# One tile fewer in the index part of a sparse attention mixer: index key and weights share a tile, and ropes, key copy and top-k rounds are reordered

## The chip, the cores and the metric

The kernel runs on one core of a Trainium2 chip. The metric is the device time of one execution in microseconds, as the median of several executions. The profile shows one execution, instruction by instruction, on TensorE (PE), VectorE (DVE), ScalarE (ACT), GpSimd (POOL) and SyncE (SP), which only issues DMAs here.

## The reference

Two transformer blocks are applied to 512 tokens of width 1024. The first has a windowed attention, a convolution and a cross attention between two feed-forward parts. The second has two layers; the first of them is the mixer that matters here:

```python
def _dsa_mixer(h, positions, w_in, q_norm_g, k_norm_g, idx_k_ln_g, idx_k_ln_b, w_out):
    proj = h @ w_in          # q 1024, k 256, v 256, qi 512, ki 64, wi 8 columns
...
    q = _rope(_rmsnorm(q, q_norm_g), positions)
    k = _rope(_rmsnorm(k, k_norm_g), positions)
    qi = _rope(qi, positions)
    ki = _rope(_layernorm(ki, idx_k_ln_g, idx_k_ln_b)[:, :, None, :], positions)[:, :, 0, :]
    wi = wi * (IDX_HEADS ** -0.5 * IDX_DIM ** -0.5)
...
        s = jnp.einsum('bqhd,bsd->bqhs', qib, ki)
        score = jnp.einsum('bqhs,bqh->bqs', jax.nn.relu(s), wib).astype(jnp.float32)
...
        _, sel = lax.top_k(score, topk)      # topk = 128
```

An index of 8 heads (queries `qi`, one shared key `ki`, weights `wi` per head) scores every earlier token for each query; the 128 best are kept, and the 16 query heads attend to these alone. `h` is a normed and modulated `x` with a shift added: `h = rmsnorm(x) * (1 + sc) + sh`.

## The kernel before

**Layout.** Activations stand feature by token: a tile is 128 features by 512 tokens. A float32 product is made of three passes, high times high, low times high and high times low, over 8 chunks of 128 rows, so a tile's job is 24 matmuls with 512 moving columns. Weights come by SP in a ring of four slots (`w_raw`); ScalarE makes the high part (`w_hi`, line 1223), and VectorE (line 1587) or, in the mixers, GpSimd (line 619, two halves) the low part. SP loads the tile j only after the split of the tile j-4.

**The mixer's tiles.** `TILES_B` lists 18 tiles of the stage `mixB`: `ki` (the 64 key columns twice, for both halves of the partitions), `wi` (8 columns), `qi0` to `qi3`, `vB0`, `vB1`, `kB0`, `kB1` and `qB0` to `qB7`. A job m computes tile m into bank m mod 4; `freed` makes it wait until the tile four before has left the bank. Between the chunks, behind chunks 2 and 5 (parts 0 and 1), `betweenB(m, part)` puts small matmuls on TensorE.

**The first two tiles.** `first_two` computes `ki` and `wi` from raw `x` before the norm is known, interleaved chunk by chunk. Their results are then scaled by the norm on VectorE (lines 2056 and 2057), and a bias, the shift times the weights, is added on ScalarE. That bias starts as eight operations per tile on VectorE, `shift_through` (lines 1627 and 1630), whose width is that of the tile, 128 and 8, in the last steps of the stage before; TensorE sums it over the partitions (line 752) ahead of the first product. Tile 2 and those after it use the normed `h`, chunk by chunk as it is made.

**The key's chain.** `ki` is centred (a total by matmul, line 1151), squared, summed (`head_sum`), its root taken on ScalarE (`head_std`), inverted on VectorE (`head_rstd`, line 1836), spread over partitions by 16 matmuls (`head_spread`, line 943, bank 5), multiplied in (`head_norm`) and roped. All spreads use bank 5, so the spread of one key waits until the norm of the key before is done (`h_normed`).

**Ropes.** `head_rope` is three VectorE operations: tile times cosine (line 1855), the tile with its halves swapped times sine (line 1857), and their sum (line 1859). The swapped tile comes by four DMAs on SP (`swap_halves`), issued in `mixer` in a fixed order between the weight loads: `qi` and `qB` seven loads behind their own, the keys nine, `ki` ten. `step_of_rope` says in which step m VectorE does it: two behind the tile for queries, four for keys, step 6 for `ki`. Staging for queries is a ring of two, so ScalarE's scaling of a query waits for the sine product of the query two before.

**Index and top-k.** `index_slot(m, part)` gives the two (block, head) pairs that TensorE scores in a part (line 1140); ScalarE applies the relu, VectorE weighs and sums it (lines 2067 and 2070). The pairs begin in job 6, part 1, and end in job 12, part 0. `take_top` is one of 16 rounds of each of three blocks of queries (256, 384 and 512 columns): the 8 largest (line 2082) and their replacement (line 2084). `TOPS_AT` says how many rounds stand ahead of the index sums of each part of a step: `{8: (0, 1), 9: (4, 1), 10: (5, 2), 11: (4, 1), 12: (0, 2), 13: (3, 0), ...}`, 33 in all; the other 15 come one per step in the attention from its step 7 on. In step m, VectorE inverts the key tile m-2 first (`head_rstd`) and norms it last (`head_norm`).

**The waits of GpSimd.** Its splits of `mixB` wait for chosen VectorE results (`qi3` roped, index sums, each `qB` roped).

## Time and profile before

| what | us |
|---|---|
| median of 3 runs | 2119.54 |
| the three runs | 2114.94, 2119.54, 2120.14 |
| profiled execution | 2114.27 |
| its span, first to last instruction | 2112.1 |
| TensorE busy in the span | 2093.0 |
| VectorE busy | 1242.8 |
| ScalarE busy | 783.1 |
| GpSimd busy | 298.9 |
| mean granted TensorE clock | 0.999 |

The span is what the trace covers; the execution's own time is 2.2 us longer. Matmul durations in the trace overlap, because each next one starts while the last one drains, so the pitch of starts tells what a matmul costs. A bracket at the end of a row is idle time of the engine ahead of it and what ended it. The stage `mixB` with its first two tiles covers about 931 to 1061 us, the attention behind it 1061 to 1169.

### The profile page before, as it was taken

The page shows a single profiled execution, that of the slowest core. Times are in us where ns is not written, and L with a number is a line of the kernel's source. Part 1 is how long each engine was busy: PE and PEld are TensorE (multiplying, and loading weights), DVE is VectorE, ACT ScalarE, POOL GpSimd, SP SyncE. Part 2 cuts the span into 40 slices and gives each one's busy share as a digit, 9 for nine tenths or more (in the row PEclk, how much of TensorE's full clock was granted, in tenths as well). Part 3 has the DMA queues.
Part 4 walks back from the last instruction along what each step waited for, and adds up shares of the span by engine and source line. Part 5 has one row for each costly group of instructions (what it writes and reads, how often), then busy time and mean ns, then how long its engine had stood idle before and what let it go on. Part 6 is the DMA issues. An engine that isn't in the chain of part 4 may idle for free.

```text
span 2112.1 us, 28230 instructions
## 1 busy us (share of the span) xinstructions
PE 2093.0 (99%) x9964; PEld 1718.3 (81%) x9968; DVE 1242.8 (59%) x1839; ACT 783.1 (37%) x1087; POOL 298.9 (14%) x357
## 2 busy tenths in 40 slices
PE   9999999999999999999999999999999999999999
PEld 7888888887888888877777888888888878888887
DVE  7666544786676654466995676654466456333332
ACT  6222333557442223334365442223343234222222
POOL 0122400650212230024300212210000000000000
PEclk9999999999999999999999999999999999999999
DMA  5556233320345542323300346542333222222232
GB/s 192 181 194 197 91 110 110 118 94 2 110 163 188 197 136 82 97 94 115 109 22 1 105 155 199 186 145 81 97 100 110 97 82 100 99 90 99 76 96 87
DMA packets 79572, 243.33 MB, mean 115 GB/s; under 512 B 12784, under 2 KB 13424, under 8 KB 79376
## 3 DMA queue, kind: packets, MB, share of 16 engines
q1 hardware_dynamic: 61376, 189.61, 27.5%
q0 software_dynamic: 18128, 52.84, 8.0%
q8 instruction: 40, 0.66, 0.1%
q14 instruction: 28, 0.23, 0.0%
HBM read 235.84 MB, written 2.29 MB: 113 GB/s over the span
## 4 chain that ended last, share of the span: by engine, by line
PE 92%; DVE 5%; ACT 1%; issue 1%; POOL 1%; DMA 0%; SPq 0%; ACTq 0%; DVEq 0%; POOLq 0%
PE ps L710 28%; PE ps L712 28%; PE ps L711 28%; PE ps L1014 2%; PE ps L972 1%; PE ps L993 1%; DVE ps L1980 1%; DVE tmp L1630 1%; DVE small L1876 1%; PE ps L975 0%; PE ps L1140 0%; POOL w_lo L619 0%; PE ps L917 0%; DVE qA L1859 0%; DVE ropA L1857 0%
## 5 line engine op out<-in xcount | busy, mean ns | idle before, releaser
L710 PE MATMUL ps<-h_hi,w_hi 128*128 128x512 f32 x1888 | 740.5, 392 | 2.8 <-issue 1.5
L712 PE MATMUL ps<-h_hi,w_lo 128*128 128x512 f32 x1888 | 735.4, 390 | 0.0
L711 PE MATMUL ps<-h_lo,w_hi 128*128 128x512 f32 x1888 | 735.2, 389 | 0.0
L1587 DVE TENSOR_TENSOR w_lo<-w_raw,w_hi 128x1024 fp32r<-128x1024 f32 x336 | 411.4, 1226 | 382.5 <-ACT w_hi L1223 368.0
L1223 ACT ACTIVATE w_hi<-w_raw 128x1024 fp32r<-128x1024 f32 x383 | 402.2, 1052 | 242.5 <-PE ps L712 240.7
L710 PEld LDWEIGHTS ps<-h_hi,w_hi 128*128 128x128 f32 x1888 | 353.8, 187 | 83.5 <-issue 8.8
L712 PEld LDWEIGHTS ps<-h_hi,w_lo 128*128 128x128 f32 x1888 | 353.7, 187 | 74.7
L711 PEld LDWEIGHTS ps<-h_lo,w_hi 128*128 128x128 f32 x1888 | 353.9, 187 | 73.1 <-issue 0.2
L710 PE MATMUL ps<-hid_hi,w_hi 128*128 128x512 f32 x704 | 274.1, 389 | 0.0
L711 PE MATMUL ps<-hid_lo,w_hi 128*128 128x512 f32 x704 | 274.0, 389 | 0.0
L712 PE MATMUL ps<-hid_hi,w_lo 128*128 128x512 f32 x704 | 274.0, 389 | 0.0
L619 POOL TENSOR_TENSOR w_lo<-w_raw,w_hi 128x512 fp32r<-128x512 f32 x100 | 132.7, 1347 | 531.4 <-ACT w_hi L1223 482.9
L1300 ACT ACTIVATE hid_hi<-tmp 128x512 f32 (+1 forms) x88 | 55.6, 632 | 393.6 <-DVE tmp L1763 384.8
L710 PEld LDWEIGHTS ps<-hid_hi,w_hi 128*128 128x128 f32 x704 | 132.2, 188 | 27.6
L711 PEld LDWEIGHTS ps<-hid_lo,w_hi 128*128 128x128 f32 x704 | 132.2, 188 | 27.3
L712 PEld LDWEIGHTS ps<-hid_hi,w_lo 128*128 128x128 f32 x704 | 132.2, 188 | 27.3
L1763 DVE TENSOR_TENSOR tmp<-tmp,ps 128x512 f32<-128x512 f32 x83 | 57.0, 687 | 132.3 <-PE ps L712 132.3
L1297 ACT ACTIVATE tmp<-ps 128x512 f32<-128x512 f32 x83 | 49.6, 598 | 223.4 <-PE ps L712 223.4
L1698 DVE SCALAR_TENSOR_TENSOR ada_sum<-ada_raw,c_act,ada_sum 128x512 f32<-128x512 f32 x168 | 125.9, 749 | 6.0 <-DMA ada_raw<-in_ada_w 1.8
L588 POOL DMA_DIRECT2D ada_raw<-in_ada_w x96 | 52.7, 549 | 393.5 <-DVE ada_sum L1698 372.8
L1704 DVE TENSOR_TENSOR hid_lo<-tmp,hid_hi 128x512 f32 (+1 forms) x88 | 61.4, 698 | 77.0 <-ACT hid_hi L1300 77.0
L1233 ACT ACTIVATE tmp<-x 128x512 f32 (+1 forms) x56 | 35.3, 631 | 158.1 <-DVE x L1609 157.7
(308 smaller groups left out, 1757.2 us busy)
## 6 DMA issues: line engine op xcount, KB each, us to landing
ada_raw<-in_ada_w POOLq DMA_DIRECT2D x96, 512.0 KB, 4.9
w_raw<-in_gate SPq DMA_DIRECT2D x88, 512.0 KB, 4.0
w_raw<-in_up SPq DMA_DIRECT2D x88, 512.0 KB, 3.5
w_raw<-in_down SPq DMA_DIRECT2D x64, 384.0 KB, 3.1
w_raw<-in_down SPq DMA_DIRECT2D x64, 320.0 KB, 2.8
w_raw<-in_w_mix_c SPq DMA_DIRECT2D x24, 512.0 KB, 3.4
w_raw<-in_w_mix_b SPq DMA_DIRECT2D x17, 512.0 KB, 3.5
w_raw<-in_w_mix SPq DMA_DIRECT2D x16, 512.0 KB, 3.5
```

The source lines that it names most:

```text
L588: pool.dma_start(ada_raw[:, (piece % 2) * 2 * ADA:(piece % 2 + 1) * 2 * ADA], src.rearrange("a p n -> (a p) n")).then_inc(ada_in[piece % 2 ...
L619: low = pool.tensor_tensor(w_lo[:, at:at + WT // 2], w_raw[:, at:at + WT // 2], f32(w_hi[:, at:at + WT // 2]), ALU.subtract)
L710: pe.matmul(dest, s_hi, m_hi, start=first and n == 0, stop=False)
L711: pe.matmul(dest, s_hi, m_lo, start=False, stop=False)
L712: mm = pe.matmul(dest, s_lo, m_hi, start=False, stop=last and n == len(pairs) - 1)
L1223: act.activation(chunk(w_hi, slot, WT), chunk(w_raw, slot, WT), ACT.Copy).then_inc(w_hi_done, 1)
L1297: act.activation(chunk(tmp, u), bank(s), ACT.Silu).then_inc(silu_done, 1)
L1300: act.activation(hid_hi[:, bass.ds(i * (2 * T) + u * T, T)], chunk(tmp, 2 + u), ACT.Copy)\
L1587: dve.tensor_tensor(chunk(w_lo, slot, WT), chunk(w_raw, slot, WT), f32(chunk(w_hi, slot, WT)), ALU.subtract).then_inc(w_lo_done, 1)
L1698: dve.scalar_tensor_tensor(ada_sum[:, :], w, c_act[:, k:k + 1], ada_sum[:, :], ALU.mult, ALU.add).then_inc(ada_sum_done, 1)
L1704: dve.tensor_tensor(hid_lo[:, at], chunk(tmp, 2 + u), f32(hid_hi[:, at]), ALU.subtract)\
L1763: dve.tensor_tensor(chunk(tmp, 2 + u), chunk(tmp, u), bank(s), ALU.mult)\
```

## The change

`ki` and `wi` share one tile: 64 key columns, 8 weight columns and 56 of zeros. The `wi` tile goes, so there are 17 jobs, and `qi0` becomes the second tile of `first_two`, computed from raw `x`, scaled by VectorE and given its bias by ScalarE. The key is handled on 64 partitions, and once normed is copied to the other 64 by a fifth DMA, for which its rope waits. The DMAs of `qi` are issued six loads behind their own instead of seven, the key's nine instead of ten; the key is roped in step 5, behind `qi2`, and its spread (8 matmuls) moves to part 1 of job 4. Index pairs begin in job 6, part 0. `kB0` and `kB1` are inverted one step earlier, behind the sums of part 0, and the table of rounds is new, with 32 rounds instead of 33 ahead of the attention. `shift_through` for the second tile is 128 wide.

```diff
-        TILES_B = ["ki", "wi", "qi0", "qi1", "qi2", "qi3", "vB0", "vB1", "kB0", "kB1"] + [f"qB{t}" for t in range(8)]
+        TILES_B = ["ki", "qi0", "qi1", "qi2", "qi3", "vB0", "vB1", "kB0", "kB1"] + [f"qB{t}" for t in range(8)]
...
         def shift_sum(n, s):
-            return tmp[:, 3 * T + s * P:3 * T + s * P + (8 if n == 3 and s == 1 else P)]
+            return tmp[:, 3 * T + s * P:3 * T + (s + 1) * P]
...
             if t == "ki":
-                return 6
+                return 5
...
-            return rot_key[t], 64
+            return rot_key[t], 80 if t == "ki" else 64
...
         def turn_bank(t):
+            if t == "wi":
+                return bank(7)[:, HD:HD + TT * 8]
...
-        TOPS_AT = {8: (0, 1), 9: (4, 1), 10: (5, 2), 11: (4, 1), 12: (0, 2), 13: (3, 0), 14: (3, 0), 15: (3, 0), 16: (3, 0),
-                   17: (1, 0)}
+        TOPS_AT = {8: (1, 4), 9: (1, 5), 10: (2, 4), 11: (1, 0), 12: (2, 0), 13: (3, 0), 14: (3, 0), 15: (3, 0), 16: (3, 0)}
...
-            at = 4 * (m - 6) + 2 * part - 2
-            return IDX[max(at, 0):at + 2] if 0 <= at < len(IDX) else []
+            at = 4 * (m - 6) + 2 * part
+            return IDX[at:at + 2] if 0 <= at < len(IDX) else []
...
+                if t == "ki":
+                    sp.dma_start(kraw[HD:P, :], kraw[0:HD, :]).then_inc(rot_sem(t)[0], 16)
...
-                    due = [t for t in tiles if has_rope(t) and j == tiles.index(t) + {"q": 7, "k": 10 if t == "ki" else 9}[t[0]]]
+                    due = [t for t in tiles if has_rope(t) and j == tiles.index(t) + {"qi": 6, "qA": 7, "qB": 7}.get(t[:2], 9)]
...
             for j in range(LEAD, len(TILES_B) + KC):
+                if j == 8:
+                    after(pool, h_roped, "qi3")
                 if j == 9:
-                    after(pool, h_roped, "qi3")
+                    after(pool, i_sum, (1, 5))
                 if j == 10:
-                    after(pool, i_sum, (1, 5))
-                if j == 11:
                     after(pool, i_sum, (2, 1))
-                if 15 <= j <= 20:
-                    after(pool, h_roped, f"qB{j - 15}")
+                if 14 <= j <= 19:
+                    after(pool, h_roped, f"qB{j - 14}")
...
-                if part == 0 and m == 5:
+                if part == 1 and m == 4:
                     head_spread("ki")
-                if part == 0 and TILES_B[m - 2] in h_normed.value and m > 4:
+                if part == 0 and TILES_B[m - 2] in h_normed.value and m > 2:
                     head_spread(TILES_B[m - 2])
...
+            after(act, d_misc, "qi_scaled")
+            act.activation(straight("qi0"), straight("qi0"), ACT.Identity, bias=shift_out(3, 1)).then_inc(h_scaled.at("qi0"), 1)
             lead(J + 1)
...
+                if t == "ki":
+                    dve.wait_ge(*rot_sem(t))
                 dve.tensor_tensor(chunk(rop, 0), straight(t), tab_cos, ALU.mult)
...
-            dve.tensor_tensor(kraw[:, :], bank(0), ssum[:, :], ALU.mult).then_inc(d_misc.at("ki_scaled"), 1)
-            dve.tensor_tensor(relu[0:8, 0:T], bank(1)[0:8, :], ssum[0:8, :], ALU.mult).then_inc(d_misc.at("wi_scaled"), 1)
+            dve.tensor_tensor(kraw[0:HD, :], bank(0)[0:HD, :], ssum[0:HD, :], ALU.mult).then_inc(d_misc.at("ki_scaled"), 1)
+            dve.tensor_tensor(features_of("wi"), bank(0)[HD:HD + 8, :], ssum[HD:HD + 8, :], ALU.mult)\
+                .then_inc(d_misc.at("wi_scaled"), 1)
+            dve.tensor_tensor(straight("qi0"), bank(1), ssum[:, :], ALU.mult).then_inc(d_misc.at("qi_scaled"), 1)
...
                 n = "ki" if m == 4 else TILES_B[m - 2]
-                if n in h_rstd.value and m > 4:
-                    head_rstd(n)
-                if m == 4:
+                if m == 3:
                     after(dve, a_misc, ("tabB", "cos"))
...
                     for b, h in index_slot(m, part):
                         index_sum(b, h)
+                    if part == 0 and TILES_B[m - 1] in ("kB0", "kB1"):
+                        head_rstd(TILES_B[m - 1])
                 if n in h_normed.value and m > 3:
                     head_norm(n, straight(n))
...
-    main = tiles(np.concatenate([ki, ki, qi, vv, k, q], axis=1))
-    wt = np.zeros((1, P, WT), np.float32)
-    wt[:, :, :KC * 8] = tiles(wi, 8)
-    a["w_mix_b"] = np.concatenate([main[0:1], wt, main[1:]], axis=0)
+    room = np.zeros((D, P - HD - 8), np.float32)
+    a["w_mix_b"] = tiles(np.concatenate([ki, wi, room, qi, vv, k, q], axis=1))
```

## Rows read from the trace of the kernel before

**Rows 1.** Page, part 1: busy time, share of the span and instructions.

```profile
PE 2093.0 (99%) x9964; PEld 1718.3 (81%) x9968; DVE 1242.8 (59%) x1839; ACT 783.1 (37%) x1087; POOL 298.9 (14%) x357
```

**Rows 2.** Windows: length, busy time per engine, granted clock, DMA share, GB/s.

```profile
977.60:1061.20 83.60, 82.91 (x426) 63.10 (x426) 74.53 (x163) 34.01 (x59) 31.59 (x24) 1.00 0.33 102
```

**Rows 3.** Timeline around the shift sums: start us, duration, engine, line, operation, idle before.

```profile
927.51 3.70 DVE L1630 SCALAR_TENSOR_TENSOR tmp<-w_raw,modc,tmp 128x8 f32<-128x8 f32 x7
...
928.09 2.57 POOL L619 TENSOR_TENSOR w_lo<-w_raw,w_hi 128x512 fp32r<-128x512 f32 x2 [0.65 <-ACT w_hi L1223]
...
931.26 0.51 PE L752 MATMUL ps<-ones,tmp 128*128 128x1 f32 x4 [0.95 <-DVE tmp L1630]
...
1561.70 2.67 DVE L1630 SCALAR_TENSOR_TENSOR tmp<-w_raw,modc,tmp 128x128 f32<-128x128 f32 x7
```

**Rows 4.** Timeline of TensorE: the first two tiles, and first products of jobs.

```profile
944.22 0.40 PE L711 MATMUL ps<-h_lo,w_hi 128*8 128x512 f32 x1
...
945.36 0.39 PE L710 MATMUL ps<-h_hi,w_hi 128*128 128x512 f32 x1
...
950.80 0.39 PE L710 MATMUL ps<-h_hi,w_hi 128*128 128x512 f32 x1
...
991.80 0.39 PE L710 MATMUL ps<-h_hi,w_hi 128*128 128x512 f32 x1
```

**Rows 5.** Timeline of TensorE: work put between the products of the jobs.

```profile
965.51 1.09 PE L943 MATMUL ps<-identity,hrB 128*64 128x128 f32 x16
...
974.24 0.70 PE L1140 MATMUL ps<-ki,qi 64*128 64x256 f32 x4
...
1002.32 1.09 PE L943 MATMUL ps<-identity,hrB 128*64 128x128 f32 x16
...
1004.33 0.92 PE L1140 MATMUL ps<-ki,qi 64*128 64x384 f32 x4
...
1012.14 1.09 PE L943 MATMUL ps<-identity,hrB 128*64 128x128 f32 x16
...
1060.09 1.05 PE L917 MATMUL ps<-matsB,hsB 128*128 128x2 f32 x8 [0.69 <-ACT hsB L1343]
```

**Rows 6.** Timeline of VectorE in the tiles of the mixer.

```profile
962.47 1.24 DVE L1857 TENSOR_TENSOR ropB<-pTB,ada_raw 128x512 f32<-128x512 f32 x1 [7.05 <-DMA pTB<-qnB]
...
996.19 2.30 DVE L2070 SCALAR_TENSOR_TENSOR score<-relu,wi,score 128x384 f32<-128x384 f32 x2 [0.30 <-ACT relu L1551]
...
1001.61 0.43 DVE L2082 MAX8 top<-score 128x8 f32<-128x256 f32 x1
...
1002.60 0.43 DVE L2082 MAX8 top<-score 128x8 f32<-128x256 f32 x1
...
1005.80 1.34 DVE L2070 SCALAR_TENSOR_TENSOR score<-relu,wi,score 128x384 f32<-128x384 f32 x2 [0.29 <-ACT relu L1551]
...
1010.50 0.68 DVE L1849 TENSOR_TENSOR pB<-pB,ps 128x512 f32<-128x512 f32 x1
...
1021.40 0.68 DVE L1855 TENSOR_TENSOR ropB<-pB,ada_raw 128x512 f32<-128x512 f32 x1
...
1023.51 0.69 DVE L1855 TENSOR_TENSOR ropB<-qnB,ada_raw 128x512 f32<-128x512 f32 x1
...
1060.74 0.69 DVE L1859 TENSOR_TENSOR qB<-ropB 128x512 f32<-128x512 f32 x1
...
1061.53 0.55 DVE L1863 RECIPROCAL qinv<-qstd 128x64 f32<-128x64 f32 x1
```

**Rows 7.** Timeline of the DMA queue and of GpSimd.

```profile
958.21 2.46 SPq L552 DMA_DIRECT2D pTB<-qnB  x4
...
992.16 5.19 POOL L619 TENSOR_TENSOR w_lo<-w_raw,w_hi 128x512 fp32r<-128x512 f32 x4 [4.31 <-DVE score L2070]
```

**Rows 8.** Timeline of VectorE in the attention: the max of a round.

```profile
1073.36 0.69 DVE L2082 MAX8 top<-score 128x8 f32<-128x512 f32 x1
```

**Rows 9.** Windows, columns as in rows 2: the stretch at low clock.

```profile
1063.00:1064.00 1.00, 1.00 (x7) 1.00 (x7) 0.97 (x4) 0.91 (x4) 0.00 (x0) 0.50 0.54 129
```

More of the change, by code:

```diff
@@ L760, in first_two @@
                         for s in range(2 * pair, 2 * pair + 2):
-                            width = 8 if n == 3 and s == 1 else P
-                            mm = product(None, bank(s)[0:width, :], [(weights(js + s, k, width),
-                                                                       (chunk(hi, k), chunk(lo, k)))], k == 0, k == KC - 1)
+                            mm = product(None, bank(s), [(weights(js + s, k), (chunk(hi, k), chunk(lo, k)))],
+                                         k == 0, k == KC - 1)
                             if k == KC - 1:
@@ L856, in freed @@
                     after(pe, v_done if tiles is TILES_B else evac, t)
-                elif t == "ki" or t[0] == "g":
+                elif t == "ki":
+                    after(pe, d_misc, "wi_scaled")
+                elif t[0] == "g":
                     after(pe, evac, t)
@@ L888, in tile_job, with turn_tile @@
                         between(m, 1)
-            def turn_tile(tiles, m):
-                t = tiles[m]
+            def turn_tile(t):
                 after(pe, evac, t)
-                if tiles is TILES_A and t != "vA":
+                if t in TILES_A and t != "vA":
                     after(pe, v_done, "vA" if t == "mv0" else "mv0")
@@ L925, in head_sum @@
                 for b in range(MT if t[:2] == "mk" else TT):
-                    mm = pe.matmul(bank(4)[:, at + 2 * b:at + 2 * b + 2],
-                                   hs[:, (n % 2) * T + b * P:(n % 2) * T + (b + 1) * P], mats[:, P:2 * P:HD],
-                                   start=True, stop=True)
+                    if t == "ki":
+                        squares, heads = hs[0:HD, (n % 2) * T + b * P:(n % 2) * T + (b + 1) * P], mats[0:HD, P:P + 2]
+                    else:
+                        squares, heads = hs[:, (n % 2) * T + b * P:(n % 2) * T + (b + 1) * P], mats[:, P:2 * P:HD]
+                    mm = pe.matmul(bank(4)[:, at + 2 * b:at + 2 * b + 2], squares, heads, start=True, stop=True)
                 mm.then_inc(sq_read.at(t), 1)
@@ L941, in head_spread @@
                 for b in range(MT if t[:2] == "mk" else TT):
-                    for half in range(2):
+                    for half in range(1 if t == "ki" else 2):
                         mm = pe.matmul(bank(5)[half * HD:(half + 1) * HD, b * P:(b + 1) * P],
@@ L1133, in index_pair @@
                     after(pe, h_roped, "ki")
+                    after(pe, v_done, "wi")
                 if pair[0][0] == 1:
@@ L1150, in betweenB @@
                     after(pe, evac, "ki")
-                    pe.matmul(bank(6), matsB[:, P:2 * P], kraw[:, :], start=True, stop=True)\
+                    pe.matmul(bank(6)[0:HD, :], matsB[0:HD, P:P + HD], kraw[0:HD, :], start=True, stop=True)\
                         .then_inc(p_misc.at("ki_total"), 1)
                 if part == 1 and m == 3:
-                    turn_tile(TILES_B, 1)
-                if part == 0 and is_token_major(TILES_B[m - 1]) and m > 2:
-                    turn_tile(TILES_B, m - 1)
+                    turn_tile("wi")
+                if part == 0 and is_token_major(TILES_B[m - 1]):
+                    turn_tile(TILES_B[m - 1])
                 if part == 0 and has_norm(TILES_B[m - 1]):
@@ L1515, in _ @@
             after(act, d_misc, "ki_scaled")
-            act.activation(kraw[:, :], kraw[:, :], ACT.Identity, bias=shift_out(3, 0)).then_inc(evac.at("ki"), 1)
+            act.activation(kraw[0:HD, :], kraw[0:HD, :], ACT.Identity, bias=shift_out(3, 0)[0:HD, :])\
+                .then_inc(evac.at("ki"), 1)
+            after(act, d_misc, "wi_scaled")
+            act.activation(features_of("wi"), features_of("wi"), ACT.Identity, bias=shift_out(3, 0)[HD:HD + 8, :])\
+                .then_inc(evac.at("wi"), 1)
+            after(act, d_misc, "qi_scaled")
+            act.activation(straight("qi0"), straight("qi0"), ACT.Identity, bias=shift_out(3, 1)).then_inc(h_scaled.at("qi0"), 1)
             lead(J + 1)
@@ L1522, in _ @@
                     head_square(t, hsB)
-                if t[:2] in ("qB", "qi"):
+                if t == "qi0":
+                    pass
+                elif t[:2] in ("qB", "qi"):
                     head_scale(t, col("g_q2") if t[:2] == "qB" else 1.0, straight(t))
@@ L1526, in _ @@
                     head_gain(t, col("g_k2"), straight(t))
-                elif t == "wi":
-                    after(act, d_misc, "wi_scaled")
-                    act.activation(features_of(t), features_of(t), ACT.Identity, bias=shift_out(3, 1)[0:8, :])\
-                        .then_inc(evac.at(t), 1)
                 else:
```

36 lines of the change are left out of this document (20 added, 16 removed).

## The prediction

> **What bounds the kernel now.** I read the page first: TensorE is busy 99% of the span [rows 1]. So whatever takes matmuls off TensorE can be worth its full time, as long as TensorE does not wait instead. Then I read the stretch from 977.6 to 1061.2 us, where most of the mixer with the index runs: TensorE is busy for 82.9 of 83.6 us and VectorE for 74.5 [rows 2]. Both numbers matter. TensorE sets the pace, but VectorE, which has the top-k rounds, is close behind. Last I read the timelines of VectorE, TensorE, GpSimd and the DMA queue around the tiles that the change touches. The reader is to see there how far behind TensorE the vector work runs, since the change takes time from TensorE and nearly none from VectorE.
>
> **The tile that goes.** The weights tile (8 columns) has 24 matmuls. With a stationary operand of 128x8 one takes 0.39 us by its row, as one of 128x128 does [rows 4]: the 512 moving columns set the time. A job of 24 takes 950.80 - 945.36 = 5.44 us [rows 4]. One job of 18 goes: -5.44 us of TensorE. The spread of the index key goes from 16 matmuls to 8; 16 take 1.09 us [rows 5], so -0.5. The matmul of the key's total keeps its 512 columns: 0. Weight bytes hardly move (a 32 KB tile goes, 17 of 512 KB stay), and one split on ScalarE and on GpSimd goes; neither engine is the bound. If nothing waited, the sum would be -5.9 us.
>
> **The shift sum.** VectorE multiplies the shift into the weights of the stage's first two tiles before TensorE may start. For the second tile this was 8 operations on 128x8 and becomes 8 on 128x128. TensorE waits on exactly this: it was idle 0.95 us until the last one had ended, at 931.26 [rows 3]. Undisturbed, seven on 128x128 take 2.67 us, 0.38 each [rows 3]. Of the seven on 128x8, two were held by GpSimd's splits at 928.09; the trace's 3.70 us are 5 of 0.24 and two of 1.2 [rows 3]. Wider operations lengthen the free five by 0.12 each: +0.6 us; if all eight lengthen by 0.14, +1.1. I take 0.6, because held ones end when GpSimd ends. Everything behind is later by it.
>
> Here a rule weighs in: the Trainium skill, GPSIMD Engine Reference, Specifications, says that GpSimd shares SBUF interfaces with VectorE and contends with instructions that have two SBUF inputs. The trace agrees: two sums on 384 columns took 2.30 us beside a GpSimd split and 1.34 without [rows 6, 7], and a sine product 1.24 us [rows 6].
>
> **Key by DMA, raw index query.** In the raw pair, VectorE and ScalarE each get one more 128x512 operation (about 0.6 us each by the rows of such operations [rows 6]); ScalarE's next split of weights is 1.3 us later (this one and the weights' bias now lie ahead of it). GpSimd's half is then ready some 0.8 us before TensorE takes that tile: hidden, and 0.5 us on the path if GpSimd is held. The rotation of a query is four DMAs that take the queue 2.46 us, and its sine product starts 962.47 - 958.21 = 4.3 us after the first issue [rows 6, 7]. qi0 is now issued at about 952.6 (behind its ScalarE operation), so rotated at 957; qi1 behind the next load at 957, rotated at 961.3 and roped at 962.6. VectorE's reciprocal for the key stands behind that rope, and TensorE now asks for it in chunk 5 of job 4, at 962.0. So TensorE waits 0.7 to 1.1 us (0.9), a wait that the trace does not have. The key is normed at 965.2; five DMAs (one more, and behind it in the queue stand qi3 and two loads) take 3.1 us, and the rope starts about 5 us behind, at 970.3, and ends at 972.4. TensorE comes to the first index pair at about 973 (before: 974.24 [rows 5]): 0, with half a microsecond to spare. The value tiles' turns and pairs only change places.
>
> **The rounds, which is where the gain goes.** Count now to the next place at which TensorE asks for a result of VectorE: the spread of kB1, job 10 part 0, which needs kB0 normed, since both use bank 5. In the kernel before (job 11 there), TensorE goes from the end of the index pair at 1004.33 + 0.92 = 1005.25 to the spread at 1012.14: 6.9 us [rows 5]. VectorE starts the sums at 1005.80 and norms kB0 from 1010.50, ending 1011.18, 1.0 ahead [rows 5, 6]. Between them stand two rounds. A round on 256 columns is 1002.60 - 1001.61 = 0.99 us [rows 6]. The new table has five rounds between them: 0.55 (pair to sum) + 1.3 (two sums) + 5 x 0.99 + 1.3 + 0.68 (norm) = 8.8 us, against 6.9 - 0.2 (a narrower pair) = 6.7 on TensorE. TensorE waits 2.1 us, and about 3 if a GpSimd split holds the second pair of sums, as it does by the order of ScalarE's splits. The reciprocals ahead of the rounds do not help, because the norm is behind the rounds.
>
> Where does this leave VectorE? The job with that pair is job 9 now. It starts at 991.8 [rows 4] + 0.6 (shift) + 0.9 (key wait) + 1.2 (net of turns, pairs, spreads and a sum that come earlier) = 994.5, so the pair ends at 999.6, and kB0 is normed at N = 1008.4 to 1009.4. Then TensorE does spread, sum and pair, 3.1 us [rows 5], VectorE adds 0.55 + 1.3, and its two rounds lie in that wait. At N + 5 = 1013.4 to 1014.4 it has done what it had done at 1011.2 before: 2.2 to 3.2 us later, not 5 earlier. It had waited for pairs in jobs 8 and 9, because few rounds now stand ahead of the sums. From there to the attention VectorE is without a gap: two ropes per kB tile and one per query at 2.1 us each (1021.40 to 1023.51) [rows 6]. It saves one round on 512 columns, moved into the attention: a max of 0.69 us [rows 8], its replace as long, and the mask's addition, 1.7 in all. Some 0.5 of order comes back. Last rope before: ends 1061.43, and the reciprocal of the queries starts at 1061.53 [rows 6]; now about 1061.5 to 1062.5.
>
> TensorE meets VectorE once more: at job 12 it needs the squares of qB2, which ScalarE makes behind relus that wait for VectorE's sums, which now stand behind two ropes (4.2 us). By the same steps VectorE has these at N + 19.7, ScalarE's square ends at N + 20.7, TensorE comes at N + 18.9: 1.8 us of waiting. The sum for TensorE up to the first scores: -5.9 + 0.6 + 0.9 + 2.6 + 1.8 = 0.0; for VectorE 0 to +1. The later of the two counts, as the first scores are 1061.15 on TensorE and the reciprocal at 1061.53: +0.5.
>
> **The moved round.** In the attention a round lies in every step from 7 on; step 22 gets one more, 1.4 us. TensorE's chunk there is bound by its own matmuls, with VectorE idle behind it: 0, and 0.7 if the mask is late for the first score on all keys.
>
> **Sum.** The profiled execution took 2114.27 us (span 2112.1, 2.2 around it): 2114.27 + 0.5 = 2114.8. The kernel's runs lie on two levels, 2114.3 and 2114.9, and 2119.5 and 2120.1, so its median of 2119.54 is 5.3 above the profiled one. With +0.5 on each level a new median is near 2115 or near 2120; I put down 2118.0, between them. A change of under 0.3% (6.4 us) can't be told from none in this kernel.
>
> **The rivals.** *A: TensorE is never kept waiting.* VectorE was busy only 89% of rows 2, had idled for 7 us ahead of 962.47, and its work starts earlier. If the waits at jobs 10 and 12 and the key's fell away, the change would be -5.9 + 0.6 = -5.3: 2109.0 profiled. Against it stands the count of five rounds. Chance 0.22. *B: slower, by the clock.* TensorE's granted clock was 0.50 in 1063 to 1064 (1.2 of 2.4 GHz) [rows 9]. Ahead of it TensorE had stood still for 0.69 us and then done only small matmuls, on 2 and 128 columns [rows 5]. The waits of 2 to 3 us at job 10 are followed by just such ones. A half-speed stretch like that one, some 3.5 us, would lose 1.7 us of products; one at job 10 and one at job 12, 3.4: 2118.2 profiled. [...] The Trainium skill, TensorE: Matmul & The Clock Gate, on oscillation, says that idle gaps between bursts bring the slow clock back; by that rule B would hold. Against it: most of each stretch is dense products. Chance 0.12. *C: the key arrives late.* If DMAs of the key land 2 us later, the first pair waits 1.5 us and all index sums with it: 2116.3. Chance 0.08. That the tile stays is excluded by the diff.
>
> **How the numbers follow.** The likeliest has 0.58; its own range is -1 to +2 us (2113 to 2116.5 profiled, 2113 to 2122 with both levels). Range: A at the lower level and B at the upper give 2109 to 2123.5; I cut 1 in 10 on each side: 2110.5 to 2122.5. Faster by over 0.3% needs A, or a median at the lower level against one at the upper: 0.20. Slower by as much needs B with more than the two stretches, or the levels the other way: 0.08. Within: 0.72.
>
> **What would show it.** Right: 17 jobs; the wide shift sums and the first product about 0.6 later; a wait of TensorE at the spread of kB1 put down to VectorE's norm of some 2 to 3 us, one at a query sum of job 12 put down to ScalarE, one below a microsecond at the key's spread; first scores near 1061 to 1062. Wrong: if TensorE has no such wait and the first scores are near 1056, it is A; if the granted clock falls within the tiles, B. My weakest step is N, for it rests on the order of short VectorE operations; a rope or a round more or less there moves the result by 1 to 2 us.

## The result, and the profile after

The changed kernel takes 2122.13 us (median of 11 runs, 2118.76 to 2128.22), beside 2115.13 us for the kernel before in the same comparison (11 runs). The ratio is 1.0033, interval 1.0024 to 1.0042: slower by 0.33%, some 7 us, where I had forecast +0.5 and no change that can be told. In a later session it gave 2124.80 (5 runs) beside 2114.55, 1.0056 (1.0042 to 1.0069). The profiled execution took 2124.55 us, its span 2122.8. Two runs of the experiments below are far longer than all others (3910.16 us, the kernel before; 5910.35 us, the key's spread later) and are left out there.

The page's chain of work that ended last, its shares by engine, says where to look: VectorE has 8% of the chain, where it had 5% before.

```profile
PE 89%; DVE 8%; issue 1%; ACT 1%; DMA 0%; SPq 0%; POOL 0%; ACTq 0%; DVEq 0%
```

TensorE still is the bound, but it now stands in the chain behind VectorE more often. The timeline of the changed kernel shows each place (start, duration, engine, line, operation, idle time before it and what ended that). First the start of the mixer, as [rows 3, 5]:

```profile
926.77 4.49 DVE L1642 SCALAR_TENSOR_TENSOR tmp<-w_raw,modc,tmp 128x128 f32<-128x128 f32 x7
...
931.31 0.61 PE L755 MATMUL ps<-ones,tmp 128*128 128x1 f32 x4 [1.79 <-DVE tmp L1642]
...
957.61 1.67 DVE L1874 TENSOR_TENSOR qi<-ropB 128x512 f32<-128x512 f32 x1
959.38 1.58 DVE L1870 TENSOR_TENSOR ropB<-qnB,ada_raw 128x512 f32<-128x512 f32 x1
961.76 0.90 DVE L1872 TENSOR_TENSOR ropB<-pTB,ada_raw 128x512 f32<-128x512 f32 x1 [0.81 <-DMA pTB<-qnB]
962.70 1.64 DVE L1874 TENSOR_TENSOR qi<-ropB 128x512 f32<-128x512 f32 x1
...
964.50 1.09 PE L949 MATMUL ps<-identity,hrB 128*64 128x128 f32 x8 [1.66 <-DVE hrB L1848]
...
975.02 0.70 PE L1147 MATMUL ps<-ki,qi 64*128 64x256 f32 x4
```

The wide shift sums cost TensorE 1.79 us of idle time, where [rows 3] have 0.95. The key's spread is 8 matmuls, as it should be, but TensorE waits 1.66 us for the key's reciprocal. Above it stands why: three operations of the ropes ahead of that reciprocal took about 1.6 us each, beside GpSimd's splits (953.9 to 966.7), where the same ones take 0.69 undisturbed [rows 6]. Of these it is the last that the reciprocal waits for: between the first two and it VectorE was idle for 0.81 us, until the turned tile had landed by DMA. At 1.64 and 0.90 us instead of 0.69 each, the last two operations bring 1.2 us. The first index pair comes at 975.02, 0.8 us behind the 974.24 of before [rows 5] and 2 us behind my 973, and did not wait for the key.

Then the place where five rounds stand ahead of the norm of kB0, and what follows:

```profile
1001.66 1.34 DVE L2087 SCALAR_TENSOR_TENSOR score<-relu,wi,score 128x384 f32<-128x384 f32 x2 [1.58 <-ACT relu L1563]
...
1007.77 2.14 DVE L2087 SCALAR_TENSOR_TENSOR score<-relu,wi,score 128x384 f32<-128x384 f32 x2
1009.84 0.68 DVE L1862 TENSOR_TENSOR pB<-pB,ps 128x512 f32<-128x512 f32 x1
...
1010.66 1.09 PE L949 MATMUL ps<-identity,hrB 128*64 128x128 f32 x16 [2.81 <-DVE pB L1862]
...
1012.67 1.83 PE L1147 MATMUL ps<-ki,qi 64*128 64x512 f32 x4
...
1015.15 0.49 DVE L2084 TENSOR_SCALAR score<-relu,wi 128x512 f32<-128x512 f32 x1 [2.80 <-ACT relu L1563]
...
1028.32 4.28 DVE L2087 SCALAR_TENSOR_TENSOR score<-relu,wi,score 128x512 f32<-128x512 f32 x4
...
1032.12 1.05 PE L921 MATMUL ps<-matsB,hsB 128*128 128x2 f32 x8 [0.95 <-ACT hsB L1351]
...
1065.35 0.49 PE L978 MATMUL ps<-kB,qB 64*128 64x128 f32 x4
```

TensorE waits 2.81 us for the norm at the spread of kB1 (no wait in [rows 5]). VectorE, which made it wait, then waits 2.80 us itself for the next pair (1015.15), and TensorE again 0.95 us for ScalarE's squares at job 12. The pair behind the first wait took 1.83 us; undisturbed it is 1.13. Why, the windows say (length; busy time of PE, PEld, DVE, ACT and POOL; granted clock, DMA share, GB/s):

```profile
1010.00:1012.00 2.00, 1.34 (x19) 1.20 (x19) 1.90 (x7) 0.00 (x0) 1.05 (x1) 1.00 0.27 64
1012.00:1014.00 2.00, 2.00 (x11) 0.95 (x10) 0.36 (x1) 0.00 (x0) 0.00 (x0) 0.74 0.43 100
1014.00:1016.00 2.00, 2.00 (x6) 1.28 (x5) 0.74 (x2) 1.08 (x2) 0.00 (x0) 0.50 0.75 260
1016.00:1018.00 2.00, 2.00 (x9) 1.30 (x9) 1.90 (x7) 0.00 (x0) 0.00 (x0) 0.91 0.01 2
...
1034.00:1036.00 2.00, 2.00 (x6) 1.52 (x6) 1.86 (x4) 0.00 (x0) 0.00 (x0) 0.50 0.47 110
...
1158.00:1160.00 2.00, 0.83 (x7) 0.69 (x7) 0.94 (x3) 1.02 (x1) 0.00 (x0) 0.93 0.00 0
1160.00:1162.00 2.00, 2.00 (x12) 2.00 (x10) 0.77 (x1) 0.00 (x0) 0.00 (x0) 0.50 0.03 8
...
1166.00:1168.00 2.00, 2.00 (x12) 2.00 (x11) 0.00 (x0) 0.00 (x0) 0.00 (x0) 0.50 0.00 0
1168.00:1170.00 2.00, 2.00 (x7) 1.61 (x7) 0.94 (x3) 0.00 (x0) 0.00 (x0) 0.51 0.00 0
...
1714.00:1716.00 2.00, 2.00 (x6) 1.61 (x5) 0.00 (x0) 0.00 (x0) 0.00 (x0) 0.50 0.76 258
```

The third number from the end is TensorE's granted clock: 0.50 (1.2 of 2.4 GHz) behind the waits at 1010.66 and 1032.12, and again at 1158 to 1170 and 1712 to 1716. A window of 2 us at 0.50 loses 1 us of TensorE's work. Summed so over all windows, the four stretches lose 1.7, 1.7, 5.1 and 1.7 us, 10.2 together; 10.28 is what the profiled execution is longer than that of before. (A fifth, at the attention's start, is in both, 1.7 us each.) The last two lie behind waits that the change did not touch. Before had the same 1.17 us wait at the attention's end, and kept the clock (its timeline and its windows):

```profile
1155.19 1.09 PE L993 MATMUL ps<-matsB,pB 128*128 128x128 f32 x8 [1.17 <-ACT pTB L1397]
```

```profile
1158.00:1160.00 2.00, 2.00 (x20) 2.00 (x19) 0.00 (x0) 0.38 (x1) 0.00 (x0) 1.00 0.00 0
```

So in these two executions the waits and the saved tile nearly cancel, and the loss is clock: the first scores come at 1065.35, 4.3 us behind the 1061.08 of before, and 3.4 of that is the clock behind the waits at 1010.66 and 1032.12. One execution each is thin evidence, and the experiments had to tell whether the order of the rounds does it.

### The profile page after: what moved, and what is told of

Its sections match the earlier page's. It is cut to its first block, busy times and chain, and to the rows that moved or that the text cites. A ratio compares the mean times of both kernels' runs of the same rounds, so it can differ in the third digit from the quotient of the medians.

```text
span 2122.8 us, 28129 instructions
## 1 busy us (share of the span) xinstructions
PE 2098.9 (99%) x9932; PEld 1724.1 (81%) x9936; DVE 1246.7 (59%) x1840; ACT 782.6 (37%) x1086; POOL 298.8 (14%) x355
## 4 chain that ended last, share of the span: by engine, by line
PE 89%; DVE 8%; issue 1%; ACT 1%; DMA 0%; SPq 0%; POOL 0%; ACTq 0%; DVEq 0%
PE ps L713 28%; PE ps L715 27%; PE ps L714 27%; PE ps L1020 2%; DVE ps L1995 1%; PE ps L978 1%; PE ps L999 1%; DVE tmp L1642 1%; PE ps L981 1%; DVE small L1891 1%; DVE score L2101 0%; DVE top L2099 0%; DVE ropA L1872 0%; PE ps L1147 0%; DVE qA L1874 0%
```

## The experiments

Each was timed beside the kernel before (2114.85, 2114.55 and 2114.55 us in the three sessions). This table has for each the median, the mean, and the mean granted clock over its runs. From the clock follows an estimate of what it cost: (1 - clock) x 2118 us. It is a rough one. The clock of a run is recorded to 0.001, which is 2.1 us of it; and over the 196 runs, each kernel and session against its own mean, the time rises by only 0.8 us for each us of the estimate. So the last two columns tell where several us are, and not one.

| kernel | runs | median | mean | mean clock | lost by clock (estimate) | rest |
|---|---|---|---|---|---|---|
| before, the three sessions of the experiments | 76 | 2114.56 | 2115.1 | 0.9985 | 3.2 | 2111.8 |
| changed, both comparisons | 16 | 2124.34 | 2123.6 | 0.9952 | 10.2 | 2113.4 |
| changed, rounds early | 12 | 2116.26 | 2117.2 | 0.9966 | 7.2 | 2110.0 |
| before, norm late | 10 | 2120.02 | 2120.1 | 0.9977 | 4.9 | 2115.2 |
| fill of 18 and 7 | 10 | 2120.41 | 2121.9 | 0.9973 | 5.7 | 2116.2 |
| fill of 11 and 3 | 6 | 2122.08 | 2121.5 | 0.9970 | 6.4 | 2115.1 |
| fill in the attention | 12 | 2118.84 | 2119.5 | 0.9969 | 6.5 | 2113.0 |
| key's spread later | 5 | 2120.20 | 2121.1 | 0.9962 | 8.0 | 2113.0 |
| shift matmuls later | 5 | 2122.33 | 2122.3 | 0.9954 | 9.7 | 2112.6 |
| all four | 11 | 2110.43 | 2111.8 | 0.9985 | 3.3 | 2108.5 |
| all four, old table | 11 | 2116.99 | 2117.4 | 0.9969 | 6.5 | 2110.8 |
| all four, sums behind ropes | 11 | 2111.89 | 2112.2 | 0.9984 | 3.5 | 2108.7 |
| all four, with fill | 11 | 2109.69 | 2111.0 | 0.9984 | 3.5 | 2107.6 |

My theory going in: the order of the rounds makes TensorE wait, and the half clock behind the waits is part of their price. Rivals: VectorE's total work is the bound wherever its rounds lie; or the loss belongs to the attention's end.

**Rounds early.** The table alone:

```
-TOPS_AT = {8: (1, 4), 9: (1, 5), 10: (2, 4), 11: (1, 0), ...
+TOPS_AT = {8: (3, 3), 9: (2, 2), 10: (4, 3), 11: (1, 0), ...
```

> The changed kernel with another table of top-k rounds alone: 10 rounds ahead of the key's norm as before 11, but two between the last pair's sums and the norm of kB0, where the changed kernel has five; the others lie in VectorE's idle time ahead of the pairs. Theory (the order of the rounds makes TensorE's waits of 2.81 us at the spread of kB1 and about 1 us at job 12, and the half clock behind each, about 1.7 us, is their consequence): the wait at the spread falls below 0.5 us, the granted clock stays 1.00 in the tiles, first attention scores near 1060.5 instead of 1065.35, time 4 to 5 us below the changed kernel. Rival 1 (VectorE's whole work up to the attention is the bound, wherever the rounds lie): the wait only moves to a later job, first scores near 1064 to 1065, time unchanged. Rival 2 (the loss lies in the attention's end, where the clock was 0.50 for 10 us): the waits go, but the median stays within 2 us of the changed kernel.

Measured: 2116.26 us, 1.0008 (0.9995 to 1.0020) of before, so 5.9 and 8.5 us below the changed kernel's two medians, more than I expected. Two rounds now stand between the pair's sums and the norm, and the spread of kB1 follows the norm without a wait:

```profile
1006.64 1.34 DVE L2087 SCALAR_TENSOR_TENSOR score<-relu,wi,score 128x384 f32<-128x384 f32 x2 [0.61 <-ACT relu L1563]
...
1011.06 0.68 DVE L1862 TENSOR_TENSOR pB<-pB,ps 128x512 f32<-128x512 f32 x1
...
1012.76 1.09 PE L949 MATMUL ps<-identity,hrB 128*64 128x128 f32 x16
...
1032.54 1.05 PE L921 MATMUL ps<-matsB,hsB 128*128 128x2 f32 x8 [0.87 <-ACT hsB L1351]
```

VectorE's own wait for the next pair fell from 2.80 to 1.02 us. By the time, both rivals fall for this part: the work on VectorE is the same, and the attention's end was not touched. The first scores alone don't decide it. They were at 1064.19, where rival 1 had put them, not at 1060.5: in this execution the clock was at 0.50 behind the shift wait (2.11 us) and the key's (1.66 us), 5.1 us in all, and the wait at job 12 was still there, 0.87. At the attention's start the clock lost 6.8 us more, and with 2122.77 us the profiled run is the second longest of its twelve. The other waits seemed worth mending too.

**The same lateness put into the kernel before.**

```
-... 10: (5, 2), 11: (4, 1), ...
+... 10: (2, 5), 11: (4, 1), ...
```

> The kernel before with one entry of the table changed: of the seven rounds of its step 10, two ahead of the first pair's sums and five behind them, so that five stand between the sums and the norm of kB0, as in the changed kernel. Theory: TensorE waits 2 to 3 us at the spread of kB1 (no wait in the kernel before), the granted clock falls to 0.50 for 2 to 4 us behind it, worth 1 to 1.7 us; VectorE is idle 2 to 3 us ahead of that; time 3 to 5 us above the kernel before. Rival (such a wait is made good later, because VectorE and not TensorE sets the attention's start): 0 to 1 us. Rival (a wait costs only itself, the clock stays): 2 to 3 us.

Measured: 2120.02 us, 1.0022 (1.0013 to 1.0031), 5.2 above before, a little more than I expected, and all ten runs between 2118.86 and 2122.16. The timeline of the two engines and the windows:

```profile
1004.65 1.34 DVE L2070 SCALAR_TENSOR_TENSOR score<-relu,wi,score 128x384 f32<-128x384 f32 x2 [3.24 <-ACT relu L1551]
...
1012.99 0.68 DVE L1849 TENSOR_TENSOR pB<-pB,ps 128x512 f32<-128x512 f32 x1
...
1013.83 1.98 PE L943 MATMUL ps<-identity,hrB 128*64 128x128 f32 x16 [2.77 <-DVE hrB L1836]
```

```profile
1014.00:1016.00 2.00, 2.00 (x18) 1.67 (x18) 1.86 (x7) 0.00 (x0) 0.19 (x1) 0.50 0.28 66
...
1022.00:1024.00 2.00, 2.00 (x7) 1.16 (x7) 0.97 (x3) 0.00 (x0) 0.00 (x0) 0.50 0.03 8
```

VectorE stands idle for 3.24 us where it had rounds to do, TensorE then waits 2.77 us for it, and the clock is at 0.50 for 10 us behind that, 5.1 us lost. The profiled run is the longest of the ten (2122.16), though, and the others lost less: by the mean clock over the ten, 4.9 us against 3.2 of before, so 1.7 more, about one short stretch. The other 3.4 us of the difference of the means are the wait and what follows from it. This is the cleanest reading of the study: moving three rounds behind a pair of sums, no work added, costs about 5 us, where the wait itself is under 3. The rival "VectorE makes it good later" falls. "A wait costs only itself", 2 to 3 us, is not quite excluded by the interval (2.7 to 6.6 us), but the clock speaks against it.

**Filling the waits with matmuls of no use.** First 18 and 7, then 11 and 3:

```
+if part == 0 and m == 10:
+    after(pe, i_relu, (2, 7))
+    idle(18, 7)          # then 11
+if part == 0 and m == 12:
+    after(pe, h_normed, "kB1")
+    idle(7, 5)           # then 3
```

> The changed kernel with matmuls of no use on TensorE ahead of the two waits: 18 on 128 columns ahead of the spread of kB1 and 7 ahead of the query sum of job 12, each about 0.12 us at full clock, so 2.2 and 0.9 us inside waits of 2.81 and 0.95 to 1.4. Theory (the half clock behind the waits is due to TensorE's standing still): granted clock 1.00 through both places, the index pair behind the spread takes half of its 1.83 us, first scores 2 to 3.4 us earlier than 1065.35, time 2 to 3.4 us below the changed kernel. Rival (the clock falls from the mix of small matmuls there, or it falls for reasons outside of the kernel): clock 0.50 there all the same, time within 1 us of the changed kernel.

> As the kernel with 18 and 7 matmuls of no use ahead of the waits at the spread of kB1 and at job 12, but with 11 and 3: the profile of that kernel shows 36 passes in 4.18 us, so one takes 0.23 us, twice the price that I had put down, and its fill was 1.3 us longer than the wait. 11 and 3 take 2.5 and 0.7 us, inside the waits of 2.81 and 0.95. Theory (in the changed kernel the clock falls behind these waits and costs 1.7 us at each): no 0.50 there, mean granted clock over the runs as high as in the longer fill (0.9973, against 0.9955 of the changed kernel), median 1.5 to 3.5 us below the changed kernel's 2122.1, so 2118.6 to 2120.6. Rival: the median stays at 2121.5 to 2122.5.

The first fill was mispriced: one such matmul is two passes in the trace, and the 18 (36 passes) took 4.18 us, 0.23 each, so that the fill outlasted the wait. Its first scores were at 1065.62, no earlier than in the changed kernel, and its median 2120.41, 1.7 and 4.4 us below the two medians of the changed kernel. The second fits (timelines of the first and the second, windows of the second):

```profile
1009.11 4.18 PE L737 MATMUL ps<-ones 128*128 128x128 f32 x36
```

```profile
1010.62 1.09 PE L949 MATMUL ps<-identity,hrB 128*64 128x128 f32 x16 [0.36 <-DVE pB L1868]
...
1031.40 1.05 PE L921 MATMUL ps<-matsB,hsB 128*128 128x2 f32 x8 [1.20 <-ACT hsB L1357]
```

```profile
1012.00:1014.00 2.00, 2.00 (x12) 1.21 (x12) 0.32 (x1) 0.21 (x1) 0.00 (x0) 1.00 0.43 99
...
1034.00:1036.00 2.00, 2.00 (x6) 1.51 (x6) 1.97 (x4) 0.00 (x0) 0.00 (x0) 0.50 0.30 70
```

With the fill the clock stayed at 1.00 behind the spread of kB1, where the changed kernel fell to 0.50 in two profiles of two. At job 12 three matmuls were too few: 1.20 us of waiting was left, and the clock fell. Over the runs the granted clock rose (0.9970 and 0.9973 against 0.9952), but of the 1.5 to 3.5 us that I expected, the medians show 0.1 to 2.7 (2122.08 against 2122.13 and 2124.80), and with six runs that is open; what the clock gave back, the rest seems to have taken (2115.1 against 2113.4). That the clock falls behind the spread of kB1 because TensorE stood still is shown, by two profiles with the fill against six of the same table without it. That filling is a cure is not: TensorE gets nothing from VectorE any earlier for it, and with the second fill its first scores came at 1064.62, only 0.7 us earlier, though the tiles lost 1.7 us less by the clock.

**Filling the wait at the attention's end.**

```
+if beside_exp == 5 and u == len(pairs) + 1:
+    idle(7, 0)
```

> The changed kernel with 7 matmuls of no use (0.9 us) ahead of the last turn of the attention, where TensorE stands still for 1.17 us in both kernels; in the changed one the profile shows the clock at 0.50 for 10 us behind it, worth 5 us. Theory (the upper of the two levels of each kernel, some 5 us apart, is this stretch, which follows the standing still in some executions and not in others): no half clock there, all runs on the lower level, near 2118.8 to 2120, median 2 to 3 us below the changed kernel. Rival (the levels come from elsewhere): runs on both levels as before, median within 1 us of the changed kernel.

Measured: 2118.84 us, 3.3 and 6 below the changed kernel's two medians, though the fill (1.78 us in its profile) is longer than the wait. Its profile has no half clock there, but that says little: of the thirteen profiles in which this wait is unfilled, only two have one, the first of the changed kernel and that of the fill of 11 and 3. Four runs of 2120.45 to 2124.00 remain, so the spread is not this one place: the profile itself lost 3.4 us behind the spread of kB1. The forecast of a single cause for the upper level was wrong, and what the lower median is due to is not shown.

**The key's spread later; the shift's matmuls later.** Each alone on the changed kernel:

```
 if k == 5:
     between(m, 1)
+if k == 7:
+    between(m, 2)        # head_spread("ki") here, m == 4
```

> The changed kernel with the spread of the index key's reciprocals on TensorE put two chunks later in job 4 (behind its last product instead of behind the sixth chunk), 1.36 us later by the products' pace. Theory (the wait of 1.66 us there is a plain loss of TensorE and gives the clock one more occasion to fall): the wait falls to about 0.3 us, the first index pair comes 1.3 us earlier unless the roped key is then late (it is ready 1.4 us ahead of it now), time 0.5 to 1.5 us below the changed kernel. Rival (what TensorE saves there it waits for at the spread of kB1 and at job 12, because VectorE's work sets both): these waits grow by as much, and the time stays within 0.5 us.

```
-if n in SHIFTED: <shift matmuls ahead of the products>
+if n == 3 and k == 5: shift_matmuls()
-TOTAL_AT (0, 1), SPREAD_AT (0, 2)
+TOTAL_AT (0, 2), SPREAD_AT (0, 3)      # n == 3
```

> The changed kernel with the two matmuls of the shift in the first tiles of this mixer behind the sixth chunk of the raw products instead of ahead of them, so that TensorE does not stand still until VectorE has the wide sums (1.79 to 2.11 us in the changed kernel, 0.95 before); the token total and the spread come one chunk later. Theory: TensorE's wait of 1.8 to 2.1 us falls below 1.2 (it next waits for the last raw half or the total, 931.8 to 933.5), the drop of the clock seen behind it in some profiles (0.50 for 2 to 8 us at 930 to 938) is rarer; time 0.7 to 2 us below the changed kernel. Rival (the wait only moves to the total): time within 0.5 us.

Both did away with most of their wait (timeline and window of the first, timeline of the second):

```profile
964.65 0.54 PE L951 MATMUL ps<-identity,hrB 128*64 128x128 f32 x3 [0.32 <-DVE hrB L1854]
...
1009.50 1.76 PE L951 MATMUL ps<-identity,hrB 128*64 128x128 f32 x16 [2.82 <-DVE pB L1868]
```

```profile
1010.00:1012.00 2.00, 2.00 (x16) 1.67 (x13) 1.13 (x4) 0.00 (x0) 0.00 (x0) 0.50 0.39 90
```

```profile
933.68 1.05 PE L731 MATMUL ps<-ones,ssum 128*128 128x1 f32 x8 [0.27 <-DVE ssum L1614]
```

0.32 us are left of 1.66, and 0.27 of 1.79. Yet against the changed kernel's 2122.13 and 2124.80 they gave 2120.20 and 2122.33 us, with five runs each; alone neither gain is told from none. The row at 1009.50 shows that the largest wait is still there: TensorE reaches the spread of kB1 1.2 us earlier and waits 2.82 us as before, and its clock is at 0.50 from 1010 on.

**All four together,** with a fourth edit for job 12: the sums of (3,4) and (3,5) between the ropes of kB0 and qB0, so that ScalarE's relus, and the squares behind them, come sooner.

```
 for r in ropes_at(TILES_B, m):
     head_rope(r, ...)
+    if m == 11 and r == "kB0":
+        for b, h in index_slot(m, 0): index_sum(b, h)
```

> The changed kernel with all of its waits for vector work mended: the table with the rounds early, the key's spread two chunks later, the shift's matmuls behind the products, and the sums of the pair (3,4) (3,5) between the rope of kB1's predecessor kB0 and that of qB0, so that ScalarE's squares for job 12 are not late. Theory (waits and the clock behind them are all of the loss, and the tile that went is worth 5.9 us): from the mean of the kernel with the rounds early, 2117.3, less 1.3 (key), 1 (shift), 0.9 (job 12) and half or all of its 3 us of excess clock loss: mean 2111 to 2114, below the kernel before (2115.5) by 1.5 to 4 us, first scores at 1057.5 to 1060. Rival (VectorE's work sets the attention's start): the waits go, the first scores stay at 1060.5 to 1061, and the time equals the kernel before within 1 us.

Measured: 2110.43 us, 0.9988 (0.9980 to 0.9997) of the kernel before: faster than it by 4 us, and than the changed one by 12 to 14. Eight of 11 runs are at or below 2111.85, and the mean of 2111.8 is in the range expected. Timeline of VectorE and TensorE:

```profile
1003.88 0.68 DVE L1872 TENSOR_TENSOR pB<-pB,ps 128x512 f32<-128x512 f32 x1
...
1005.58 1.09 PE L955 MATMUL ps<-identity,hrB 128*64 128x128 f32 x16
...
1055.82 0.49 PE L984 MATMUL ps<-kB,qB 64*128 64x128 f32 x4
```

The first scores come at 1055.82, 5.3 us ahead of the 1061.08 of before: nearly all of the 5.9 us that the tile and the spread are worth, and earlier than I had put them. So VectorE's total work does not hold them at 1060.5; the rival falls. In the tiles this profile has no half clock. The wait for the key's reciprocal is 0.44 us here, but 1.57 in the three kernels built on this one below, where the sine product ahead of it took 1.45 to 1.79 us instead of 0.69. Hundredths of a microsecond decide it: here the sine product began at 961.08, just ahead of the next of the splits on GpSimd (961.09), and with the old table at 961.04, just behind one (960.99).

**What each is worth inside of it.** The changed kernel again, then the four less the table, less the sums, and with a fill in one more wait:

> The changed kernel once more, unchanged, beside the three others on one chip. Theory: TensorE's waits are the same to 0.3 us (1.8 to 2.1 at the shift, 1.66 at the key's spread, 2.8 at the spread of kB1, 0.9 to 1.3 at job 12), but the stretches of clock 0.50 lie behind others of them and have other lengths than in the first profile, and the times spread over 8 us or more with the mean clock: median 2119 to 2124. Rival (the half clock belongs to fixed places of this program): the same four places as in the first profile, behind the waits at 1010.66, 1032.12, 1159.45 and 1711.45.

> The kernel with all four mendings less the one of the rounds: the changed kernel's own table, with five rounds ahead of the norm of kB0. Theory (the rounds ahead of the norm are most of the loss): TensorE waits 2.8 us or more at the spread of kB1 and loses the clock there, time 5 to 8 us above the kernel with all four (2110.4), so 2115.5 to 2118.5. Rival (the four small waits share the loss evenly): 2 to 3 us above it.

> The kernel with all four mendings less that of job 12: the sums of (3,4) (3,5) are again behind both ropes. Theory: a wait of 0.9 to 1.5 us for ScalarE's squares at job 12 and now and then half clock behind it, time 1 to 3 us above the kernel with all four: 2111.4 to 2113.4. Rival (the wait is hidden, since VectorE is as late): within 0.5 us of it.

> The kernel with all four mendings and 9 matmuls of no use on 128 columns (2.1 us at 0.23 each) in TensorE's wait of 2.34 us ahead of the last projection, behind which the clock was 0.50 for 3.4 us in its profile, and in four of the eight other profiles. Theory (standing still is what lets the clock fall): clock 1.00 there, time 0.5 to 1.5 us below the kernel without them, more runs at a mean clock of 0.999. Rival: the clock falls there all the same, or later, and the time stays.

The changed kernel again, TensorE at a key spread of the first mixer and in the tiles, and a window:

```profile
458.70 1.12 PE L949 MATMUL ps<-identity,hrA 128*64 128x128 f32 x8 [2.68 <-DVE hrA L1848]
...
1017.20 1.09 PE L949 MATMUL ps<-identity,hrB 128*64 128x128 f32 x16 [2.83 <-DVE pB L1862]
```

```profile
460.00:462.00 2.00, 2.00 (x10) 2.00 (x11) 1.12 (x5) 0.26 (x1) 0.00 (x0) 0.50 0.75 256
```

Its waits are those of the first profile (2.11, 1.66, 2.83; at job 12 only 0.34). The clock fell behind other ones: at 458 to 466, behind a wait of 2.68 us that was 0.94 in the kernel before and in the first profile of the changed one; at the first tiles; behind the spread of kB1, as before; but neither at job 12 nor at the attention's end nor ahead of the last projection. So the places vary, and the rival of fixed places falls, but for the spread of kB1. The median, 2124.80, is 0.8 us above the range that I had given, and the five runs spread over 7.3 us. The old table in the kernel with all four:

```profile
1009.50 1.09 PE L955 MATMUL ps<-identity,hrB 128*64 128x128 f32 x16 [2.82 <-DVE pB L1872]
```

Measured: 2116.99 us against 2110.43. The rounds alone are worth 6.6 us of the 12 to 14, as the theory had it. The sums behind the ropes: 2111.89 us, 1.5 above, a wait of 0.86 us at job 12; the time is inside the forecast, but the means differ by only 0.4 us, so these runs don't tell it from none. The fill ahead of the last projection: 2109.69 us, 0.7 below, and 0.9983 (0.9973 to 0.9992) of before. The rows say that 2.34 us of waiting became 0.34, with matmuls of no use in the rest, and the clock was kept there:

```profile
1695.24 2.17 PE L737 MATMUL ps<-ones 128*128 128x128 f32 x18
1697.75 0.49 PE L713 MATMUL ps<-y_hi,w_hi 128*128 128x512 f32 x1 [0.34 <-DVE y_lo L2203]
```

One profile says little here too: of the thirteen in which this wait is unfilled, seven have half clock behind it (I had counted four of eight) and six have none. Nor is the gain the clock's: the mean clock is that of the kernel without the fill (0.9984 and 0.9985), and runs at 0.999 or more are 5 of 11 against 6 of 11. A gain of 0.7 us by this fill is not shown.

## Why the prediction was wrong

The sum of waits was right to 0.3 us, with errors in its terms that cancel, and its price was not right. By its own steps:

- The tile, -5.44, and the spread, -0.5: right to 0.6 by the all-four kernel, whose first scores are 5.3 us earlier than before.
- Shift sums, +0.6 forecast: 0.84 (1.79 - 0.95), 1.2 in three other profiles of the same code (2.11).
- Wait for the key's reciprocal, 0.9 (0.7 to 1.1) forecast: 1.66. I let the rope ahead of it run undisturbed, though I had given the held sine product of [rows 6] in the same text.
- Key at the first pair, 0: right. The key was not late (rival C falls).
- Wait at the spread of kB1, 2.1, or near 3 with GpSimd's hold: 2.81, with that hold (sums of 2.14 us at 1007.77). Counting the five rounds was right. The time N at which kB0 is normed, my weakest step, came out at 1010.5, 1.1 us behind my range; TensorE came later too, so the wait did not feel it.
- Wait at job 12, 1.8 forecast: 0.95, and 0.15 to 1.26 in four other profiles with the changed table and no fill. Mechanism right, size half of the forecast.
- TensorE up to the first scores, 0.0 forecast: -5.94 + 0.84 + 1.66 + 2.81 + 0.95 = +0.3 by these rows.
- The moved round, 0: from first scores to the first product behind the attention it is 98.9 us in the all-four kernel (1055.82 to 1154.73), 98.7 before (1061.08 to 1159.78). Right to 0.2.

The step that failed is the one that charged each wait its own length and kept the clock out of the likeliest case: the sum of +0.5 has no term for it. "B: slower, by the clock" had the place (jobs 10 and 12) and the price of one stretch (1.7 us) as the profile then showed them, and I gave it 0.12, because "most of each stretch is dense products". The profile of before could not settle that reason: its clock fell behind a wait of only 0.69 us with small matmuls behind it [rows 5, 9], and stayed at 1.00 behind one of 2.37 us with dense products behind it. The changed kernel's fell in dense products too (1712 to 1716 is the last projection). B as written, 3.4 us, was right for the two places in the first profile and too small for the runs. Over 16 runs the mean granted clock fell from 0.9985 to 0.9952, 7.0 us by the estimate of the table, or 5.6 at 0.8 us for each of them, of a difference of the means of 8.5. The rest, 1.6 to 2.9 us, is what my +0.5 speaks of. Rival A (TensorE never waits, -5.3) is not what the change did, but it is near what it could have done: the all-four kernel is 4.1 us faster than the kernel before.

That 2122.13 still lies at the edge of my range, 2110.5 to 2122.5, is luck. That end came from the upper of two levels that I read out of three runs. Of eleven runs of the kernel before, nine lie between 2114.20 and 2115.85 and two at 2119.54 and 2120.14, so my own sum pointed to about 2115.6 (2115.13 + 0.5), and the 2118.0 was no reading of anything. And a change of under 0.3% can be told: with eleven runs each the interval was 0.1% to either side.

The Trainium skill (TensorE: Matmul & The Clock Gate, HAM oscillation) says that idle gaps between bursts bring the slow clock back. I cited it and let dense products outweigh it. The runs agree with the page that the clock falls behind gaps, and show it behind shorter ones than those of its example: 1.17, 1.20, 1.66, 2.8 us. They also show that it is no certainty (1.17 and 2.37 us without a fall before).

What stays open: why the clock falls behind a given wait in one execution and not in the next, and so whether the falls outside of the tiles (5.1 and 1.7 us in the first profile after, none in that of before, 3.4 elsewhere in the second) came more often because of the change. That the clock was lost behind the spread of kB1 in every profile with that wait unfilled, seven of seven, is shown (changed twice, before with the late norm, attention fill, key's spread later, shift later, old table); in the five without that wait (the kernel before is one) and the two with it filled, it stayed. Behind other waits it fell more rarely, counted over the profiles that have them unfilled: the last projection's 2.34 or 2.37 us, 7 of 13; the shift's 1.79 to 2.11, 4 of 7; those of 0.86 to 1.26 at job 12, 3 of 6; the attention's end, 1.17, 2 of 13; the key's reciprocal, 1.57 to 1.70, 1 of 10. The length of the wait alone does not sort them, and what does was not tested.

## What to carry to other kernels

When a table spreads filler work among dependent steps, read for each entry which result stands behind it and who waits for that: filler belongs ahead of a hand-over that isn't ready yet, never between the ready input and the result that the bound engine asks for. Two engines that feed each other can both stand still for one such misplacement (2.81 us of TensorE, then 2.80 of VectorE here). Mending one of several waits can show nothing in a few runs until the largest is gone. Where profiles show the granted clock falling behind waits, put a wait down at its length plus a share of what a half-clock stretch costs in a profile of the same kernel, and compare means of the granted clock over many runs, not the clock of one profile.

## What the runs showed of the hardware

- In the kernel before with the late norm a wait of 2.77 us came with 5.2 us in the median (each of ten runs was at least 4.0 above that of before). TensorE ran at 0.50 for 10 us behind it in the profile; over the runs the clock took about 1.7 us more than before. Stretches of half clock lost 1.7, 3.4 or 5.1 us by the windows, and once 6.8 (rounds early, at 1064 to 1080), and not by the length of the wait ahead of them: 5.1 behind 1.17 us, 1.7 to 5.1 behind 2.8.
- The time of a run follows its mean granted clock: 2118.8 at 0.998 and 2128.2 at 0.993 in the changed kernel. Over 196 runs, each kernel and session against its own mean, the two go together with a correlation of 0.90.
- Beside GpSimd's splits VectorE's operations on two tiles take longer: two sums on 384 columns took 1.34 us alone, 2.14 to 2.31 beside a split, and 3.20 in one profile (rounds early, splits from 998.26 to 1006.55):

```profile
1000.99 3.20 DVE L2087 SCALAR_TENSOR_TENSOR score<-relu,wi,score 128x384 f32<-128x384 f32 x2
```
